# First feed-forward layer of a DiT step: row chunks of the modulation weights on two DMA queues, squares per token, and four weight tiles multiplied part by part

## The chip, the cores and the metric

One core of a Trainium2 chip runs the whole kernel. The metric is the device time of one execution in microseconds (us). The engines named below are TensorE (PE in the views, with PEld for its weight loads), VectorE (DVE), ScalarE (ACT), GpSimd (POOL) and SyncE (SP). SP and ACT also issue DMAs: SP on queue q1, ACT on queue q10. Both queues use the same 16 DMA engines.

## The reference, cut to what matters

One layer is computed for 128 prompt tokens and 512 sample tokens, 640 in all, of width 1024. The change touches only its start: the modulation vectors, the first norm, and the first products of the first feed-forward network. The two groups of tokens have their own conditioning (`c_ctx` and `c`), so every modulation value exists twice.

```python
def adaln(cond, w_ada, b_ada):                     # w_ada: 1024 x 9216, nine vectors of 1024
    m = jax.nn.silu(cond) @ w_ada + b_ada
    return m.reshape(cond.shape[:-1] + (1, N_MOD, D_MODEL))

def modulated_norm(x, gain, shift, scale):
    return rmsnorm(x, gain) * (1 + scale) + shift  # rmsnorm: x * rsqrt(mean(x*x) + EPS) * gain

x = x + 0.5 * mod[..., 2, :] * swiglu(modulated_norm(x, norm_ffn1, mod[..., 0, :], mod[..., 1, :]),
                                      w_ffn1_in, w_ffn1_out)
```

The first norm needs only the modulation vectors 0 and 1 (shift and scale), which are the first 2048 columns of `w_ada`, 8 MB. `swiglu` multiplies the result with `w_ffn1_in` (1024 x 5632: 22 gate and 22 up tiles of 128 columns) and then with `w_ffn1_out`.

## The kernel before, in words

Tokens lie in the free dimension: `x_t` is [128, 8, 640], eight blocks of 128 features (`KD` = 8) by 640 tokens (`T`), and a half is 320 tokens (`HT`). Each fp32 product is made of three matmuls of rounded parts (`w_lo`·`h_hi`, `w_hi`·`h_lo`, `w_hi`·`h_hi`), lines 2234 to 2236, the function `product`. A weight tile [128, 1024] is loaded into `w_raw` (two buffers), ACT rounds it to `w_hi` (`w_high`, line 718) and DVE subtracts to get `w_lo` (`w_low`, line 1330). A part of the norm is one feature block of one half; there are 16. For each part DVE multiplies by the root (`scale_x`, line 1367), ACT applies scale and shift (`modulate`, line 770), and DVE splits the result (`split_h`, lines 1376 and 1377).

The order on each engine is the order in which the code is written, and engines meet only through semaphores. At the start it is this:

- SP issues twelve small loads (lines 509 to 515: identity, biases, conditioning, gains), then `x_tok` (lines 516 and 517), then `w_ada` in column pieces: ten `ada_tiles` of 128 columns and three `ada_wide` of 256 columns, each over all 1024 rows (lines 523 and 525), then the first weight tiles (line 531).
- PE turns the small rows, turns the 40 blocks of `x_tok` into `x_t` (line 2527; ACT copies them out, line 993), multiplies the ten `ada_tiles` with the conditioning (function `ada`, line 2281), sums the squares over features with a matmul by 1/D (`mean`, line 2254), sums the partitions of the three `ada_wide_acc` (`ada_sum`, line 2290), and turns the rows of modulation values into columns (line 2543).
- DVE multiplies the three wide pieces (`ada_setup`, lines 1460 and 1464) and adds up the squares between the first and the second (`add_square`), then makes `w_low` of tiles 0 and 1, `mods` (line 1771) and `scales` (line 1358).
- ACT copies `x_t` out, squares it by feature block (`square_of`, line 725), takes the root (`root`, lines 742 and 744), and makes `w_high` of tiles 0 and 1 and the copies `ada_row` (line 1005).

Then the 16 parts run, and PE multiplies tiles 0 and 1 part by part as they come (`by_parts`). Tiles 2 and 3 get their `w_high` and `w_low` at parts 9 and 15, in slots of their own at the end of the space of `act_lo`. PE multiplies them whole afterwards (`hidden(1, ...)`), and goes on with tiles 4, 5 and so on. Beside it DVE and ACT make the activation of pair `j` (function `hidden` on both), and DVE multiplies two pieces of `w_ada` per pair for the later modulation vectors (`ada_part`, `ada_fold`).

Of the kernel before, what the change touches and what calls it, by code (L numbers as in the profile page):

```python
# [14 lines left out]
P = 128  # L15
# [63 lines left out]
ADA_PE, ADA_DVE = 10, 3  # L79
SQ_BASE, PART_BASE = [0, 8, 12, 16], [None, 0, 4]  # L80
# [185 lines left out]
def hybrid_step(nc, x_prompt, x_sample, cache_diff_k, cache_diff_v, state_delta, c, c_ctx, w_ada, b_ada,  # L266
# [4 lines left out]
    with ctx:  # L271
# [43 lines left out]
        with ExitStack() as s:  # L315
            tb = holder(s)
            x_tok = tb("x_tok", [P, NT, D])

            ada_tiles = [tb(f"ada_tile{i}", [P, D]) for i in range(ADA_PE)]
            ada_row = tb("ada_row", [2, ADA_PE * P])  # L320
            ada_wide = [tb(f"ada_wide{i}", [P, 2 * D]) for i in range(ADA_DVE)]
            rows_a = tb("rows_a", [120, P])
            rows_b = tb("rows_b", [62, P])
        with ExitStack() as s:
            holder(s)("act_space", [P, 2 * NJ * T])
            ada_wide_acc = [holder(s)(f"ada_wide_acc{i}", [P, 2 * PAIR]) for i in range(ADA_DVE)]
        with ExitStack() as s:
# [10 lines left out]
            fold = tb("fold", [P, P])  # L338
            ada_sums = rstd
# [103 lines left out]
        ada_landed = [sem(f"ada_landed{i}") for i in range(ADA_PE)]  # L443
        ada_wide_in = [sem(f"ada_wide_in{i}") for i in range(ADA_DVE)]
        ada_wide_read, ada_rows = sem("ada_wide_read"), sem("ada_rows")
# [55 lines left out]

        @block.sync
        def _(sp):
# [12 lines left out]
            sp.dma_start(x_tok[:, 0, :], x_prompt[0]).then_inc(x_in, 16)  # L516
            sp.dma_start(x_tok[:, 1:NT, :], x_sample[0].rearrange("(t p) d -> p t d", p=P)).then_inc(x_in, 16)
            ada_v = w_ada[0].rearrange("(k p) n -> p k n", p=P)

            for n in range(ADA_PE):  # L520
                if n % 3 == 0 and n // 3 < ADA_DVE:
                    col = ADA_PE * P + n // 3 * PAIR
                    sp.dma_start(ada_wide[n // 3][:].rearrange("p (k n) -> p k n", k=KD),
                                 ada_v[:, :, col:col + PAIR]).then_inc(ada_wide_in[n // 3], 16)
                sp.dma_start(ada_tiles[n][:].rearrange("p (k n) -> p k n", k=KD),  # L525
                             ada_v[:, :, n * P:(n + 1) * P]).then_inc(ada_landed[n], 16)

# [182 lines left out]
        def _(act):  # L710
# [272 lines left out]

            act.wait_ge(cols_turned, 2)
# [4 lines left out]
            nc.scalar.activation(cond[:, :, 0], cols_a[:, 80:88], ACT.Silu).then_inc(cond_ready, 1)  # L989
            for i in range(2 * NT):  # L990
                t, q = i // 2, i % 2
                act.wait_ge(x_turned, i + 1)
                nc.scalar.copy(x_t[:, 4 * q:4 * q + 4, t * P:(t + 1) * P], heads4(ps[:, 2 + i % 4, :], P)).then_inc(x_copied, 1)
            act.wait_ge(x_copied, 2 * NT)
            load_power_table()
            for k in range(KD):
                square_of(k, 0, None)
            root(0, 0)
            root(0, 1)
            w_high(0, 0)  # L1000
            w_high(1, 1)
            act.wait_ge(ada_used, ADA_PE)
            for n in range(0, ADA_PE, 4):
                end = min(n + 4, ADA_PE)
                ins = nc.scalar.copy(ada_row[:, n * P:end * P], ps[0:2, 4 + n // 4, 0:(end - n) * P])
            ins.then_inc(ada_rows, 1)
            for s in range(16):
                modulate(0, s)
                if s in (9, 15):
                    i = 2 if s == 9 else 3  # L1010
                    w_high(i, i % 2, slot=i, done=0)
# [311 lines left out]
        def _(dve):  # L1323
# [63 lines left out]
            def update_half(nth, i, gate, half):  # L1387
# [9 lines left out]
                elif nth == 1 and half == 0:  # L1397
                    dve.wait_ge(half_done[0], i + 1)
                    if i == 0:
                        dve.wait_ge(ada_summed, ADA_DVE + 3)  # L1400
# [97 lines left out]
            def first_ffn():  # L1498

                def hidden(j, par, first=False):  # L1500
# [9 lines left out]
                    if isinstance(j, int) and j == NJ - 1:  # L1510
                        dve.wait_ge(ada_summed, ADA_DVE + 2)
# [245 lines left out]
            def ada_setup(i):  # L1757
                dve.wait_ge(ada_wide_in[i], 16)
                ada_terms(ada_wide_acc[i], ada_wide[i], range(KD), 0, KD - 1).then_inc(ada_wide_read, 1)

            dve.wait_ge(cond_ready, 2)
            ada_setup(0)
# [7 lines left out]
            dve.wait_ge(ada_summed, ADA_DVE + 1)  # L1770
            own.link(nc.vector.tensor_tensor(mods[:, 0:2 * KD, :], ps[:, 7, 0:4 * KD].rearrange("p (m a) -> p m a", a=2),
                                             spread(cols_a[:, 0:2 * KD], 2), ALU.add))
# [3 lines left out]
            for s in range(16):  # L1776
# [3 lines left out]
                if s in (9, 15):  # L1780
                    i = 2 if s == 9 else 3
                    w_low(i, i % 2, slot=i)
# [446 lines left out]
        def _(pe):  # L2229
# [17 lines left out]
            def mean(nth, half):  # L2247

                if nth == 0:
                    pe.wait_ge(sq_added, SQ_BASE[1])  # L2250
                else:
                    pe.wait_ge(added_half[half], PART_BASE[nth] + len(PARTS[nth]))
                bank = half if nth == 0 else 4 + half
                nc.tensor.matmul(ps[:, bank, 0:HT], ones_d[:], half_of(sumsq, half), start=True, stop=True).then_inc(mean_mm, 1)
# [22 lines left out]
            def ada(n):  # L2277

                pe.wait_ge(ada_landed[n], 16)
                for a in range(KD):  # L2280
                    ins = nc.tensor.matmul(ps[0:2, 4 + n // 4, (n % 4) * P:(n % 4 + 1) * P], cond[:, a, :],
                                           ada_tiles[n][:, a * P:(a + 1) * P], start=(a == 0), stop=(a == KD - 1))
                ins.then_inc(ada_used, 1)

            def ada_sum(bank, at, acc):

                for u in range(2):
                    for g in range(2):
                        c = at + 2 * u + g
                        ins = nc.tensor.matmul(ps[:, bank, c:c + 1], acc[:, g * PAIR + u * P:g * PAIR + (u + 1) * P],  # L2290
                                               ones_col[:], start=True, stop=True)
                ins.then_inc(ada_summed, 1)
# [6 lines left out]
            def first_ffn():  # L2299
# [65 lines left out]
                by_parts(0, [0, 1], [0, 1], False)  # L2365
                hidden(1, 1, 2)
# [619 lines left out]
```

## Time and profile before

| | us |
|---|---|
| runs before | 1584.05, 1586.75, 1586.85 |
| median of them | 1586.75 |
| the profiled execution | 1581.51 |
| its span in the trace | 1579.7 |
| PE busy in the span | 1523.3 (96%) |
| DVE, ACT, POOL busy | 1062.2, 591.4, 196.2 |
| moved by DMA | 141.96 MB, of it 118.26 MB on SP's queue |

The profile is of one execution on the chip. Its span is 1.8 us shorter than that execution's time, and that execution is 5.2 us shorter than the median. Times below count from the span's start. PE is busy nearly throughout, so the span is PE's work plus the time in which PE waits. Engines other than PE count where PE waits for them.

### The profile page before, as it was taken

Reading aid. Unit: us, or ns where it says so; the run is one execution under the profiler, and the core shown is the slowest. Engines: PE = TensorE matmul, PEld = TensorE weight load, DVE = VectorE, ACT = ScalarE, POOL = GpSimd, SP = SyncE. Lnnn points to the kernel's source line nnn. Section 1 sums busy time; section 2 is a strip of 40 time slices with the busy share of each in tenths; the row PEclk is TensorE's granted clock in tenths of the full one; section 3 lists DMA queues with packets and bytes.
Section 4 is the critical chain, followed back from the end, with each engine's and each line's share of the span. In section 5 each row is a group of like instructions: output and inputs, shape, how many; then the busy total and the mean of one; then the engine's idle time right before and its main releaser. Section 6 shows DMA issues by size and latency. Waiting matters only on the chain.

```text
span 1579.7 us, 26562 instructions
## 1 busy us (share of the span) xinstructions
PE 1523.3 (96%) x10204; PEld 1435.9 (91%) x10204; DVE 1062.2 (67%) x1908; ACT 591.4 (37%) x1138; POOL 196.2 (12%) x158
## 2 busy tenths in 40 slices
PE   6899999999999999998998999999999999999998
PEld 4899999999999999987887988999999999998886
DVE  5978777787374767554867887678887777763334
ACT  4522222221122533533653214264554444444323
POOL 0000000000000000020006677566000000000000
PEclk9999999999999999999997999999999999999999
DMA  9354454544244312211001101002213322222222
GB/s 303 118 158 142 140 158 148 156 143 157 83 138 147 94 54 67 68 46 49 28 28 34 41 15 28 21 28 83 65 41 94 94 80 80 80 80 67 72 75 94
DMA packets 186937, 141.96 MB, mean 90 GB/s; under 512 B 8544, under 2 KB 169829, under 8 KB 186725
## 3 DMA queue, kind: packets, MB, share of 16 engines
q1 hardware_dynamic: 164149, 118.26, 24.4%
q10 hardware_dynamic: 22704, 22.55, 4.5%
q8 instruction: 57, 0.93, 0.2%
q14 instruction: 27, 0.22, 0.1%
HBM read 137.34 MB, written 3.45 MB: 89 GB/s over the span
## 4 chain that ended last, share of the span: by engine, by line
PE 86%; DVE 7%; SPq 2%; ACT 2%; issue 1%; POOL 1%; DMA 1%; DVEq 0%; ACTq 0%
PE ps L2234 14%; PE ps L2236 14%; PE ps L2235 14%; PE ps L2396 5%; PE ps L2398 5%; PE ps L2397 5%; PE ps L2468 3%; PE ps L2467 3%; PE ps L2466 3%; PE ps L2898 3%; PE ps L2902 3%; SPq L525 2%; PE ps L2669 1%; PE ps L2905 1%; PE ps L2690 1%
## 5 line engine op out<-in xcount | busy, mean ns | idle before, releaser
L2234 PE MATMUL ps<-h_hi,w_lo 128*128 128x320 f32 x1152 | 364.0, 316 | 9.3 <-DVE h_lo L1377 4.0
L2236 PE MATMUL ps<-h_hi,w_hi 128*128 128x320 f32 x1152 | 356.4, 309 | 0.0
L2235 PE MATMUL ps<-h_lo,w_hi 128*128 128x320 f32 x1152 | 356.4, 309 | 0.0
L1330 DVE TENSOR_TENSOR w_lo<-w_raw,w_hi 128x1024 fp32r<-128x1024 f32 x120 | 147.6, 1233 | 232.0 <-ACT w_hi L718 231.7
L2234 PEld LDWEIGHTS ps<-h_hi,w_lo 128*128 128x128 f32 x1152 | 216.9, 188 | 15.9 <-DVE h_lo L1377 6.9
L2235 PEld LDWEIGHTS ps<-h_lo,w_hi 128*128 128x128 f32 x1152 | 217.1, 188 | 0.8 <-issue 0.2
L2236 PEld LDWEIGHTS ps<-h_hi,w_hi 128*128 128x128 f32 x1152 | 216.7, 188 | 0.0
L718 ACT CAST w_hi<-w_raw 128x1024 fp32r<-128x1024 f32 x120 | 125.6, 1048 | 207.1 <-PE ps L2236 109.5
L1464 DVE SCALAR_TENSOR_TENSOR ada_acc<-ada_ffn,cond,ada_acc 128x256 f32<-128x256 f32 x392 | 161.8, 478 | 1.2
L2234 PE MATMUL ps<-act_hi,w_lo 128*128 128x320 f32 (+1 forms) x352 | 108.9, 309 | 2.1 <-DVE mods L1493 2.1
L2236 PE MATMUL ps<-act_hi,w_hi 128*128 128x320 f32 (+1 forms) x352 | 108.5, 308 | 0.0
L2235 PE MATMUL ps<-act_lo,w_hi 128*128 128x320 f32 (+1 forms) x352 | 108.5, 308 | 0.0
L2396 PE MATMUL ps<-h_hi,w_lo 128*128 128x320 f32 x304 | 94.0, 309 | 0.6 <-ACT sumsq L882 0.6
L2398 PE MATMUL ps<-h_hi,w_hi 128*128 128x320 f32 x304 | 93.9, 309 | 0.0
L2397 PE MATMUL ps<-h_lo,w_hi 128*128 128x320 f32 x304 | 93.7, 308 | 0.0
L2466 PE MATMUL ps<-w_hi,act_hi 128*128 128x512 f32 x220 | 87.4, 397 | 0.0
L2468 PE MATMUL ps<-w_hi,act_lo 128*128 128x512 f32 x220 | 86.8, 395 | 0.0
L2467 PE MATMUL ps<-w_lo,act_lo 128*128 128x512 f32 x220 | 86.8, 394 | 0.0
L812 ACT CAST act_hi<-scratch 128x640 f32 (+1 forms) x22 | 16.0, 728 | 148.2 <-DVE scratch L1519 148.2
L2234 PEld LDWEIGHTS ps<-act_hi,w_lo 128*128 128x128 f32 x352 | 66.1, 188 | 2.4 <-issue 2.3
L2235 PEld LDWEIGHTS ps<-act_lo,w_hi 128*128 128x128 f32 x352 | 66.1, 188 | 0.1
L2236 PEld LDWEIGHTS ps<-act_hi,w_hi 128*128 128x128 f32 x352 | 66.1, 188 | 0.0
(384 smaller groups left out, 3200.4 us busy)
## 6 DMA issues: line engine op xcount, KB each, us to landing
w_raw<-in_w_ffn_in SPq DMA_DIRECT2D x64, 512.0 KB, 3.8
w_raw<-in_w_ffn_out SPq DMA_DIRECT2D x44, 512.0 KB, 3.7
ada_ffn<-in_w_ada ACTq DMA_DIRECT2D x43, 512.0 KB, 3.5
w_raw<-in_w_in SPq DMA_DIRECT2D x28, 512.0 KB, 3.7
ada_ffn<-in_w_ffn_in SPq DMA_DIRECT2D x20, 512.0 KB, 3.7
ada_ffn<-in_w_ada SPq DMA_DIRECT2D x13, 512.0 KB, 4.5
ada_tile<-in_w_ada SPq DMA_DIRECT2D x10, 512.0 KB, 7.8
w_raw<-in_w_out SPq DMA_DIRECT2D x8, 512.0 KB, 3.4
```

The costliest lines, as they stand in the source:

```text
L718: nc.scalar.copy(w_hi[s if slot is None else slot], w_raw[s][:]).then_inc(w_hi_ready, 1)
L1330: nc.vector.tensor_tensor(w_lo[at], w_raw[s][:], w_hi[at].bitcast(F32), ALU.subtract)\
L1464: ins = nc.vector.scalar_tensor_tensor(a, w, col, a, op0=ALU.mult, op1=ALU.add)
L2234: nc.tensor.matmul(out, lo, xh, start=start, stop=False)
L2235: nc.tensor.matmul(out, hi, xl, start=False, stop=False)
L2236: return nc.tensor.matmul(out, hi, xh, start=False, stop=stop)
L2396: nc.tensor.matmul(out, lo, xh, start=start and k == 0, stop=False, skip_group_check=not start)
L2397: nc.tensor.matmul(out, hi, xl, start=False, stop=False, skip_group_check=not start)
L2398: ins = nc.tensor.matmul(out, hi, xh, start=False, stop=k == 3, skip_group_check=not start)
L2466: nc.tensor.matmul(out, lo, wh, start=first, stop=False)
L2467: nc.tensor.matmul(out, hi, wl, start=False, stop=False)
L2468: ins = nc.tensor.matmul(out, hi, wh, start=False, stop=last)
```

## The change

The loads. `w_ada` is now read in eight chunks of 128 rows by 2048 columns (`ada_k`, `head_load`), 1 MB each, so that one row of a chunk is 8 KB in one piece. ACT issues chunks 0, 1 and 2, then `x_tok`, then chunk 3, ahead of all its other work. SP issues the twelve small loads as before, then chunk 4, `fold`, weight tile 0, chunk 5, weight tile 1, chunks 6 and 7.

The modulation values. Of every chunk PE multiplies the first 1152 columns (`ada`, three matmuls per chunk, summed in PSUM over the chunks), and DVE the other 896 (`ada_chunk`, two instructions per chunk). One transposing reduction on DVE and one matmul by `fold` take the place of the 12 matmuls by `ones_col`.

The norm. The squares are taken per token from `x_tok` with a sum along the row (five instructions), the root is five columns, and six matmuls of a broadcast column with the identity (`HEAD_SPREAD`) spread it over the partitions; ACT copies it to `rstd`.

The products. `first_parts(4)` multiplies four weight tiles: at step `s` tiles 0 and 1 with part `s`, tiles 2 and 3 with part `s - 4`. `hidden(1, ...)` is gone. `w_high` and `w_low` of tiles 2 and 3 stand at parts 1 and 2 of ACT, 2 and 3 of DVE, where they stood at 9 and 15.

```diff
@@ sync: before                                    @@ after
-            sp.dma_start(x_tok[:, 0, :], x_prompt[0]).then_inc(x_in, 16)
-            sp.dma_start(x_tok[:, 1:NT, :], x_sample[0].rearrange("(t p) d -> p t d", p=P)).then_inc(x_in, 16)
...
+            for k in range(4, KD):
+                head_load(sp, k)
+                if k == 4:
+                    sp.dma_start(fold[:], consts[:, N_SMALL:N_SMALL + P]).then_inc(fold_in, 16)
+                if k in (4, 5):
+                    ffn_load(k - 4)
+            for i in range(2, 4):
+                ffn_load(i)
@@ scalar
+            for k in range(3):
+                head_load(act, k)
+            act.dma_start(x_tok[:, 0, :], x_prompt[0]).then_inc(x_in, 16)
+            act.dma_start(x_tok[:, 1:NT, :], x_sample[0].rearrange("(t p) d -> p t d", p=P)).then_inc(x_in, 16)
+            head_load(act, 3)
...
+            for t in range(NT):
+                ins = nc.scalar.activation(x_tok[:, t, :], x_tok[:, t, :], ACT.Square, accum_out=tok_rs[:, t:t + 1])
...
             w_high(0, 0)
+            for half in range(2):
+                act.wait_ge(mean_mm, half + 1)
+                nc.scalar.copy(half_of(rstd, half), ps[:, half, 0:HT]).then_inc(rstd_ready, 1)
             w_high(1, 1)
@@ vector
             for k in range(KD):
-                add_square(k, 0)
-            ada_setup(1)
-            ada_setup(2)
-            w_low(0, 0)
-            w_low(1, 1)
+                ada_chunk(k)
+                if k in (4, 5):
+                    w_low(k - 4, k - 4)
+            own.wait_back(0)
+            nc.vector.tensor_reduce(head_sums[:], ada_wide_acc[:].rearrange("p (n r) -> p n r", r=32), AX.X, ALU.add,
+                                    apply_transpose=True).then_inc(ada_wide_read, 1)
@@ tensor
+            def first_parts(lag):
+                for s in range(2 * KD + lag):
+                    for m in range(4):
+                        p = s if m < 2 else s - lag
+                        if not 0 <= p < 2 * KD:
+                            continue
+                        half, k = divmod(p, KD)
+                        if m == 0:
+                            pe.wait_ge(h_ready, p + 1)
+                        if p == 0:
+                            pe.wait_ge(w_lo_ready, m + 1)
...
-                by_parts(0, [0, 1], [0, 1], False)
-                hidden(1, 1, 2)
+                first_parts(4)
...
+            pe.wait_ge(cond_ready, 2)
+            for a in range(3):
+                ada(a)
             pe.wait_ge(x_in, 32)
             for i in range(2 * NT):
                 t, q = i // 2, i % 2
-                if i >= 4:
-                    pe.wait_ge(x_copied, i - 3)
+                if i in (7, 9):
+                    ada(3 if i == 7 else 4)
+                if i >= len(HEAD_BANKS):
+                    pe.wait_ge(x_copied, i - len(HEAD_BANKS) + 1)
```

Where instructions stand. On DVE at the start, of the kernel before: the wide pieces, the sums of squares between them, and both `w_lo` after them, ahead of `mods`.

```order
L1460 TENSOR_SCALAR ada_wide_acc<-ada_wide,cond 128x256 x2
L1464 SCALAR_TENSOR_TENSOR ada_wide_acc<-ada_wide,cond,ada_wide_acc 128x256 x14
L1339 COPY sumsq<-square 128x640
L1342 TENSOR_TENSOR sumsq<-sumsq,square 128x640 x7
...
L1330 TENSOR_TENSOR w_lo<-w_raw,w_hi 128x1024 x2
L1771 TENSOR_TENSOR mods<-ps,cols_a 128x32
```

On DVE at the start, of the changed kernel, from the first chunk to the first `scratch` of the norm:

```order
L1779 TENSOR_SCALAR ada_wide_acc<-ada_k,cond 128x896 x2
L1782 SCALAR_TENSOR_TENSOR ada_wide_acc<-ada_k,cond,ada_wide_acc 128x896 x8
L1345 TENSOR_TENSOR w_lo<-w_raw,w_hi 128x1024
L1782 SCALAR_TENSOR_TENSOR ada_wide_acc<-ada_k,cond,ada_wide_acc 128x896 x2
L1345 TENSOR_TENSOR w_lo<-w_raw,w_hi 128x1024
L1782 SCALAR_TENSOR_TENSOR ada_wide_acc<-ada_k,cond,ada_wide_acc 128x896 x4
L1791 TENSOR_REDUCE head_sums<-ada_wide_acc 128x56
L1795 TENSOR_TENSOR mods<-ps,cols_a 128x18
L1801 TENSOR_TENSOR mods<-ps,cols_a 32x14 x4
L1373 SCALAR_TENSOR_TENSOR scales<-mods,cols_a 128x16
```

The two `w_lo` have moved from behind the last wide piece to between chunks 4 and 5 and between chunks 5 and 6, so three chunks and the reduction now stand behind the first of them. The sums of squares are gone from DVE.

On ACT at the start, of the changed kernel, from the issue of its six loads to the copies `ada_row`; each wait is in brackets. Before, its first row was the copy `cols_a`, and the squares stood behind ten copies of `x_t` as here.

```order
L506 DMA ada_k<-in_w_ada 128x2048 x3
L989 DMA x_tok<-in_x_prompt 128x1024
L990 DMA x_tok<-in_x_sample 128x4x1024
L506 DMA ada_k<-in_w_ada 128x2048
...
L1002 COPY x_t<-ps 128x4x128 [waits x_turned] x10
L1005 ACTIVATE x_tok,tok_rs<-x_tok 128x1024 [waits x_turned]
L1005 ACTIVATE x_tok,tok_rs<-x_tok 128x1024 x4
L1010 ACTIVATE tok_rs<-tok_rs,eps_col 128x5 [waits ones_set,sq_tok]
L1012 ACTIVATE tok_rs<-tok_rs 128x5 [waits log_ready]
L722 CAST w_hi<-w_raw 128x1024 [waits w_landed0]
L1016 COPY rstd<-ps 128x320 [waits mean_mm] x2
L722 CAST w_hi<-w_raw 128x1024 [waits w_landed1]
```

The load of `x_tok` has moved from SP to ACT and stands behind three chunks of 1 MB. The first `w_hi`, for which the first `w_lo` on DVE waits, stands behind the squares and the root, as it did before.

## Rows read from the trace of the kernel before

**Rows 1.** Windows, three stretches: start:end, length, busy (instructions), PEclk, DMA share, GB/s.

```profile
0.00:48.14 48.14, 30.00 (x241) 24.10 (x241) 29.13 (x68) 22.48 (x38) 0.21 (x4) 0.96 0.86 275
48.14:67.46 19.32, 17.94 (x97) 15.42 (x98) 18.72 (x46) 13.66 (x23) 0.00 (x0) 0.93 0.28 90
67.46:1579.70 1512.24, 1475.35 (x9870) 1396.39 (x9868) 1014.32 (x1796) 555.23 (x1078) 195.98 (x154) 0.99 0.27 84
```

**Rows 2.** Chain of waits of the start: start, length, what.

```profile
35.23 6.50 DMA w_raw<-in_w_ffn_in
```

**Rows 3.** Timeline, SP: start, length, issue.

```profile
0.75 0.38 SPq L509 DMA_DIRECT2D ident<-in_consts  x1
...
4.63 0.25 SPq L515 DMA_DIRECT2D rows_b<-in_diff_norm  x1
4.93 0.36 SPq L516 DMA_DIRECT2D x_tok<-in_x_prompt  x1
```

**Rows 4.** Timeline, PE: start, length, instruction, [idle before it, released by].

```profile
5.89 0.46 PE L2519 MATMUL ps<-ident,rows_a 120*128 120x120 f32 x1 [5.89 <-DMA rows_b<-in_diff_norm]
...
13.77 6.06 PE L2527 MATMUL ps<-ident,x_tok 128*128 128x128 f32 x40 [7.13 <-DMA x_tok<-in_x_sample]
21.03 8.89 PE L2281 MATMUL ps<-ada_tile,cond 128*2 128x128 f32 x80 [1.20 <-ACT x_t L993]
```

**Rows 5.** Windows, DMA rate of two stretches: `x_tok`, then column pieces of `w_ada`.

```profile
8.00:14.00 6.00, 0.23 (x1) 0.23 (x2) 0.00 (x0) 0.66 (x3) 0.00 (x0) 1.00 1.02 401
17.00:29.00 12.00, 10.80 (x100) 8.82 (x98) 11.20 (x22) 10.74 (x17) 0.00 (x0) 1.00 1.13 359
```

**Rows 6.** Timeline, ACT at the start.

```profile
8.48 0.19 ACT L989 ACTIVATE cond<-cols_a 128x8 f32<-128x8 f32 x1
...
16.63 4.14 ACT L993 COPY x_t<-ps 128x512 f32<-128x512 f32 x8 [0.27 <-PE ps L2527]
...
41.75 1.04 ACT L718 CAST w_hi<-w_raw 128x1024 fp32r<-128x1024 f32 x1 [0.43 <-DMA w_raw<-in_w_ffn_in]
```

**Rows 7.** Groups by form, ACT, whole run: busy us, mean ns | idle before.

```profile
L754 ACT ACTIVATE square<-x_fin 128x512 f32<-128x512 f32 x10 | 6.3, 629 | 4.9 <-DVE x_fin L1445 4.6
...
L754 ACT ACTIVATION_READ_ACCUMULATOR square<-x_fin 128x1 f32 x10 | 1.9, 186 | 0.0
...
L1315 ACT ACTIVATE sums_fin<-sums_fin 128x1 f32<-128x1 f32 x5 | 1.5, 295 | 0.5
```

**Rows 8.** Timeline, DVE at the start.

```profile
17.13 5.63 DVE L1464 SCALAR_TENSOR_TENSOR ada_wide_acc<-ada_wide,cond,ada_wide_acc 128x256 f32<-128x256 f32 x14
...
41.94 2.35 DVE L1330 TENSOR_TENSOR w_lo<-w_raw,w_hi 128x1024 fp32r<-128x1024 f32 x2
45.37 0.19 DVE L1771 TENSOR_TENSOR mods<-ps,cols_a 128x32 f32<-128x32 f32 x1 [1.08 <-PE ps L2543]
```

**Rows 9.** Groups by form, DVE, whole run.

```profile
L1798 DVE SCALAR_TENSOR_TENSOR conv_acc<-pre,cols_b,conv_acc 128x642 f32<-128x642 f32 x48 | 42.6, 888 | 5.2 <-DVE conv_acc L1798 3.3 <-DVE conv_acc L1796 1.1
...
L1464 DVE SCALAR_TENSOR_TENSOR ada_wide_acc<-ada_wide,cond,ada_wide_acc 128x256 f32<-128x256 f32 x42 | 16.9, 480 | 0.0
...
L1484 DVE TRANSPOSE_TENSOR_REDUCE rstd<-ada_acc 128x16 f32<-128x512 f32 x12 | 8.5, 712 | 0.4
```

**Rows 10.** Timeline, PE: first products, and tile 2 at its start and eight products later.

```profile
48.14 0.64 PE L2234 MATMUL ps<-h_hi,w_lo 128*128 128x320 f32 x1 [2.88 <-DVE h_lo L1377]
...
50.97 0.31 PE L2235 MATMUL ps<-h_lo,w_hi 128*128 128x320 f32 x1
...
67.46 0.31 PE L2234 MATMUL ps<-h_hi,act_lo 128*128 128x320 f32 x1
...
70.97 0.31 PE L2234 MATMUL ps<-h_hi,act_lo 128*128 128x320 f32 x1
```

**Rows 11.** Timeline, DVE after the norm: activation of pair 0.

```profile
72.26 0.81 DVE L1519 TENSOR_TENSOR scratch<-square,ps 128x640 f32<-128x640 f32 x1
...
76.03 2.35 DVE L1330 TENSOR_TENSOR w_lo<-w_raw,w_hi 128x1024 fp32r<-128x1024 f32 x2
```

More of the change, by code:

```diff
@@ L325, in hybrid_step @@
             holder(s)("act_space", [P, 2 * NJ * T])
-            ada_wide_acc = [holder(s)(f"ada_wide_acc{i}", [P, 2 * PAIR]) for i in range(ADA_DVE)]
+            ada_wide_acc = holder(s)("ada_wide_acc", [P, 2 * ADA_WIDE * P])
         with ExitStack() as s:
@@ L992, in _ @@
                 act.wait_ge(x_turned, i + 1)
[L993 to L999, printed above, removed]
+                nc.scalar.copy(x_t[:, 4 * q:4 * q + 4, t * P:(t + 1) * P], heads4(ps[:, HEAD_BANKS[i % len(HEAD_BANKS)], :], P)).then_inc(x_copied, 1)
+            act.wait_ge(x_turned, 2 * NT)
+            for t in range(NT):
+                ins = nc.scalar.activation(x_tok[:, t, :], x_tok[:, t, :], ACT.Square, accum_out=tok_rs[:, t:t + 1])
+            ins.then_inc(sq_tok, 1)
+            act.wait_ge(sq_tok, 1)
+            act.wait_ge(ones_set, 1)
+            rs = tok_rs[:, 0:NT]
+            nc.scalar.activation(rs, rs, ACT.Ln, bias=eps_col[:], scale=1.0 / D).then_inc(log_ready, 1)
+            act.wait_ge(log_ready, 1)
+            nc.scalar.activation(rs, rs, ACT.Exp, scale=-0.5).then_inc(log_ready, 1)
             w_high(0, 0)
+            for half in range(2):
+                act.wait_ge(mean_mm, half + 1)
+                nc.scalar.copy(half_of(rstd, half), ps[:, half, 0:HT]).then_inc(rstd_ready, 1)
             w_high(1, 1)
-            act.wait_ge(ada_used, ADA_PE)
             for n in range(0, ADA_PE, 4):
                 end = min(n + 4, ADA_PE)
+                act.wait_ge(ada_used, n // 4 + 1)
                 ins = nc.scalar.copy(ada_row[:, n * P:end * P], ps[0:2, 4 + n // 4, 0:(end - n) * P])
@@ L1008, in _ @@
                 modulate(0, s)
-                if s in (9, 15):
-                    i = 2 if s == 9 else 3
-                    w_high(i, i % 2, slot=i, done=0)
+                if s in (1, 2):
+                    w_high(s + 1, (s + 1) % 2, slot=s + 1, done=0)
             first_ffn()
@@ L1773, in _ @@
+            dve.wait_ge(ada_summed, HEAD_SUMS)
+            for q in range(4):
+                rows = slice(32 * q, 32 * q + 32)
+                sums = ps[rows, 3, 0:8 * ADA_WIDE].rearrange("p (g u q) -> p u g q", g=2, q=4)[:, :, :, q]
+                own.mark(nc.vector.tensor_tensor(mods[rows, ADA_PE:2 * KD, :], sums, spread(cols_a[rows, ADA_PE:2 * KD], 2), ALU.add))
+            own.wait_back(0)
             make_scales(0)
@@ L2275, in by_parts, with ada @@
                             mean(nth, 1)
[L2277 to L2292, printed above, removed]
+            def first_parts(lag):
[9 more added lines that the diff above has]
+                            pe.wait_ge(w_lo_ready, m + 1)
+                        w = (w_hi[m][:, k * P:(k + 1) * P], w_lo[m][:, k * P:(k + 1) * P])
+                        x = [half_of(h[k // 4][:, k % 4, :], half) for h in (h_hi, h_lo)]
+                        ins = product(ps[:, 2 * m + half, 0:HT], k, w, x, k == 0, k == KD - 1)
+                        if p == 2 * KD - 1:
+                            ins.then_inc(tile_done, 1)
+            def ada(a):
+                pe.wait_ge(ada_landed[a], 16)
+                for i, n in enumerate((512, 512, ADA_PE * P - 1024)):
+                    ins = nc.tensor.matmul(ps[0:2, 4 + i, 0:n], cond[:, a, :], ada_k[a][:, i * 512:i * 512 + n],
+                                           start=(a == 0), stop=(a == KD - 1))
+                    if a == KD - 1:
+                        ins.then_inc(ada_used, 1)
             def ada_fold(col, i0, i1):
@@ L2544, in _ @@
             ins.then_inc(ada_summed, 1)
+            pe.wait_ge(fold_in, 16)
+            pe.wait_ge(ada_wide_read, 1)
+            nc.tensor.matmul(ps[:, 3, 0:8 * ADA_WIDE], fold[:], head_sums[:], start=True, stop=True).then_inc(ada_summed, 1)
             first_ffn()
```

95 lines of the change are left out of this document (46 added, 49 removed).

## The prediction

> **What bounds the kernel now.** I cut the span into stretches first. From 67.46 on PE is busy 1475 of 1512 us [rows 1], and the change leaves that stretch's work alone except for the first pairs. Before 48.14 PE is busy 30 us, but none of it is a product; from 48.14 to 67.46 it multiplies tiles 0 and 1. So the question is by how much the first product at 48.14, and then the start of tile 4, come earlier or later. I call the first product's time F.
>
> The chain of waits says what sets F today: SP's queue. It ends on the landing of weight tile 1, which `w_hi` waits for until 41.75 [rows 2, 6]. From 8 to 14 us the queue delivers 401 GB/s with the DMA engines full (share 1.02), and from 17 to 29, in pieces of 512 B and 1 KB, 359 GB/s with a share of 1.13 [rows 5]. Before the first product 12.1 MB must land: 8.39 of `w_ada`, 2.62 of `x_tok`, 1.05 of two weight tiles. `x_tok` stands in front and has landed at 13.77 [rows 4]. Not far behind the queue is DVE, which works without a gap from 17.1 to 44.3 [rows 8].
>
> **What the change gives in bytes.** 8 KB rows are nearest to the 4 KB rows of `x_tok`, so I take 401 GB/s for everything. 12.1 MB is then 30.2 us. A load's lead (issue, first byte, last receipt) is what `x_tok` shows: issued at 4.93, landed at 13.77, 8.84 us for 6.54 us of bytes, so 2.3 us [rows 3, 4]. ACT's first issue can stand at 0.75, like SP's today. All would have landed at about 33.5 instead of 41.7. The Trainium skill ("DMA: Bandwidth & Descriptors", section "Issuing engines are not separate DMA queues") says that DMAs of two engines interleave on the same 16 DMA engines and that a second issuer saves only issue time. The share of 1.02 on one queue [rows 5] agrees, and the 33.5 already counts one bandwidth for both queues.
>
> **What it costs in order.** If only bytes counted, F would come from the last chunk: two DVE instructions, the reduction, the fold, `mods` and the first part, near 41. But `x_tok` no longer stands in front. I call its landing X and follow what hangs on it.
>
> 1. *Copies.* From X to the last copy of `x_t` takes 7.0 us today (13.77 to 20.77, [rows 4, 6]). PE now also multiplies chunks 3 and 4 between the blocks: 40 products of 128 columns take 8.89 us, 0.222 each, so 9 x 0.222 = 2.0 us a chunk [rows 4]; ACT's backlog hides some 0.5 of the 4.0. X + 10.5.
> 2. *Squares.* Five of 1024 columns. One of 512 takes 0.63, and reading its sum 0.19 [rows 7]; a cast of 1024 takes 1.04 [rows 6], twice the 512 would be 1.26. I take 1.05 + 0.19 less 0.1 of overlap, 1.14 each, 5.7 in all (5.2 to 7.2). X + 16.2.
> 3. *Root.* Two instructions on five columns, 0.30 and below [rows 7], with hand-overs 0.65. X + 16.85.
> 4. *`w_high(0)`*: 1.04 [rows 6]. X + 17.9. It was hidden behind loads before.
>
> On DVE the wait that matters is new: `w_low(0)` waits for this `w_high(0)`, and behind it on DVE stand chunks 5, 6 and 7, `w_low(1)`, the reduction, `mods` and the norm. PE waits for the norm. Their prices:
>
> 5. Two `w_low`, 2.35 [rows 8].
> 6. Three chunks, six instructions of 896 columns. 256 columns take 0.480, 642 take 0.888 [rows 9], so 1.06 ns a column and 1.16 for 896; back to back 14 of 256 take 5.63, 0.40 each [rows 8, 9], 0.08 less than alone. 6 x 1.08 = 6.5.
> 7. The reduction: 0.71 for 512 columns [rows 9]; with the same slope 2.1 for 1792 (1.9 to 2.5).
> 8. The fold matmul with hand-overs, 0.4, an estimate: 56 columns are under the 0.22 of 128 [rows 4].
> 9. From `mods` at 45.37 to the first product at 48.14 it takes 2.77 today [rows 8, 10]; four more small additions cost 0.4 (one takes 0.19 alone). 3.2.
> 10. Hand-overs on DVE, 0.3.
>
> Together 14.85, so **F = X + 32.7**. `w_high(1)`, the `rstd` copies and `ada_row` lie beside steps 5 and 6. `w_low(1)` needs `w_high(1)` about 2.2 after `w_high(0)`, and DVE comes to it 3.4 after. Chunk 0 to 4's work on DVE lies in front of the wait and costs nothing, nor do the additions of squares that went.
>
> **X.** Ahead of it and in it on ACT's queue are 3.15 + 2.62 = 5.77 MB. No stretch of this trace has two full queues, so I bound it. If ACT's queue is served alone: 0.75 + 2.3 + 14.4 = 17.4. If both queues get the same bytes from 7.2 on, when chunk 4 (issued in `x_tok`'s old place at 4.93) flows, 1.67 MB have gone and 4.1 MB take 20.5 us: 27.7. Between: both queues take turns row by row. Chunk rows are 8 KB, rows of `x_tok` 4 KB, rows of a weight tile 512 B. ACT's 1.5 MB of chunks then goes beside chunk 4's 1.05 MB; after it SP's small rows take little, about 0.35 MB of `fold` and tile 0. X = 17.4 + 1.4/0.401 = 20.9. I take 20.9: it needs no rank among the queues and lies between the bounds, nearer to the one with ACT's head start. F = 53.6, 5.5 later than 48.14.
>
> **Four tiles.** Today tiles 0 and 1 end at 67.46, and a product takes 0.439 (eight from 67.46 to 70.97), so tiles 2 and 3 end at 81.5, F + 33.4 [rows 10]. A part comes every 1.2 us (16 in 19.3, [rows 1]) and PE, with two products of 0.88 each, waits for it. After: parts 2 and 3 carry both `w_low` (2.35) and ACT's two `w_high`, so part 4 comes at about F + 7.3, with eight products done; its waits hide the slow start, in which today ten matmuls take 2.83 instead of 1.47 [rows 10]. From there four products a step, 1.76, outlast the norm's 1.2, and the other 56 products take 24.6: F + 31.9. Then tile 4. Its `w_low` stands on DVE behind the activation of pair 0, and from there to its end took 72.26 to 77.2, 4.95 us [rows 11]. Today a whole pair of tiles (14 us) covers it. Now tiles 0 and 1 end only at about F + 27.6; with 0.4 until DVE can start, `w_lo` is there at F + 33.0, and PE waits 1.1. Net 0.4 gained, nought to 2 in the range.
>
> **Sum.** 5.5 - 0.4 = 5.1 later. The profiled execution would take 1581.5 + 5.1 = 1586.6. The median stands 5.2 above it, and I carry that over: 1586.75 + 5.1 = 1591.9, so 1592.
>
> **Rivals.**
> - *ACT's queue goes first* (no change). Place: the 16 DMA engines between 7 and 21 us. If chunk 4 and tile 0 don't hold `x_tok` up, X = 17.4 and F = 50.1; 2.0 - 0.4 = 1.6 later, 1588.4. It decides below X = 18.9, where the loss is 3.2. For it: ACT's loads are all issued by 3.5, before SP's big ones. Against it: nothing in the trace gives one queue a rank.
> - *Equal bytes.* X = 27.7, and chunk 3, which PE wants at X + 4, lands with the last of SP's at 33 and costs 1.3 more. F = 61.7: 13 later, 1600.
> - *The small loads come late.* SP's twelve small loads, landed at 5.89 today [rows 4], now meet a full ACT queue. If each of them waits behind a chunk, they land with ACT's 6.8 MB, near 20; `cond` is ready 2.8 after them (8.67, [rows 4, 6]), PE multiplies chunks 0 to 2 for 6 us ahead of the blocks, and X counts as 28: F = 60.7, 12 later, 1599. The Trainium skill ("DMA: Bandwidth & Descriptors", section "Queues, rings and completion order") says that each DMA engine goes round the queues packet by packet, a packet being some 9 to 17 descriptors; a chunk has 8 rows per DMA engine, so by that rule this rival holds. No run here shows it, and the sum above does without it.
> - *Faster.* X = 17.4, the short squares (0.5), the short reduction (0.2) and 2 us from four tiles together: F = 49.4, and 0.7 us gained, 1586. More than that needs a price that I have wrong: the wait of `w_low(0)` gone, which would leave the bytes as the bound, F near 41 and 1579.
>
> **How the numbers follow.** A measurement of this kernel tells 0.2%, 3.2 us, from no change. Row by row 0.44 (1592), ACT first 0.20 (1588.4, no change), small loads late 0.13 (1599), equal bytes 0.13 (1600), faster cases 0.10, of which 0.02 lie within 3.2. That gives slower 0.70, same 0.22, faster 0.08. The range runs from 1585 to 1601: it leaves out most of the faster cases and the upper end of equal bytes.
>
> **What would show it.** In the changed profile: `x_tok` lands between 17 and 28, and PE's idle time before its blocks names it. DVE idles before the first `w_lo`, released by ACT's `w_hi`, though chunk 5 has landed. The first product comes near X + 33. There is a short PE gap before tile 4, released by DVE's `w_lo`. I am wrong if DVE goes through `w_lo` without idling, if `x_tok` lands before 16, or if F is below 48.

## The result, and the profile after

The changed kernel takes 1588.27 us (median of 12 runs, 1586.33 to 1592.33), the kernel before 1586.13 (12 runs, 1582.52 to 1588.37). The ratio of the runs is 1.0025, 95% interval 1.0015 to 1.0035: 4.0 us slower, 2.4 to 5.6; the two medians by themselves lie 2.1 apart. That lies in the forecast range and on the forecast side. The profiled execution took 1586.57 with a span of 1584.8, 5.1 us more than before. The sum had said 5.1.

TensorE's own row first, the timeline of PE after (start, length, instruction, idle before it and who ended it). It answers [rows 4, 10]: the small rows turned, the chunks multiplied, the blocks of `x_tok`, the fold, the first product, part 4 and tile 4.

```profile
11.67 0.46 PE L2553 MATMUL ps<-ident,rows_a 120*128 120x120 f32 x1 [11.67 <-DMA rows_b<-in_diff_norm]
...
14.51 7.69 PE L2324 MATMUL ps<-ada_k,cond 128*2 128x512 f32 x18 [2.08 <-ACT cond L997]
22.13 3.27 PE L2566 MATMUL ps<-ident,x_tok 128*128 128x128 f32 x28
...
49.39 0.65 PE L2585 MATMUL ps<-head_sums,fold 128*128 128x56 f32 x2 [5.29 <-DVE head_sums L1791]
53.41 0.63 PE L2263 MATMUL ps<-h_hi,w_lo 128*128 128x320 f32 x1 [3.38 <-DVE h_lo L1392]
60.61 0.41 PE L2263 MATMUL ps<-h_hi,w_lo 128*128 128x320 f32 x1 [0.86 <-DVE h_lo L1392]
86.65 0.41 PE L2263 MATMUL ps<-h_hi,w_lo 128*128 128x320 f32 x1 [1.14 <-DVE w_lo L1345]
```

F is 53.41 (forecast 53.6), part 4 stands at F + 7.2 (7.3), tile 4 at F + 33.2 (33.0) behind a gap of 1.14 (1.1). Before, tile 4 started at 81.54, so the start costs 5.1 us. The span is 5.1 longer: nothing behind tile 4 adds to it or gives it back.

The loads, as the groups of DMA issues after (KB each, us from issue to landing). ACT issued the prompt at 2.17 and the sample at 2.90:

```profile
x_tok<-in_x_sample ACTq DMA_DIRECT2D x1, 2048.0 KB, 17.6
...
x_tok<-in_x_prompt ACTq DMA_DIRECT2D x1, 512.0 KB, 12.5
```

X, the landing of `x_tok`, is 20.5 (forecast 20.9; before 13.77). The bytes go as fast as hoped, by the windows after (start:end, length, busy of PE, PEld, DVE, ACT, POOL, then PEclk, DMA share, GB/s), which answer [rows 5]:

```profile
8.00:12.00 4.00, 0.33 (x1) 0.18 (x1) 0.00 (x0) 0.00 (x0) 0.00 (x0) 1.00 1.02 426
20.00:24.00 4.00, 4.00 (x26) 2.38 (x24) 0.72 (x2) 1.18 (x3) 0.00 (x0) 1.00 1.04 402
...
28.00:32.00 4.00, 3.32 (x16) 1.15 (x14) 0.00 (x0) 1.97 (x4) 0.00 (x0) 1.00 1.01 428
32.00:36.00 4.00, 3.78 (x12) 0.85 (x10) 0.00 (x0) 4.00 (x9) 0.00 (x0) 1.00 0.07 31
```

From 32 on the queues are nearly empty: the last load, chunk 7, landed at 33.2, where before the last one landed at 41.7. DVE could have gone on. Its timeline after shows why it didn't, and answers [rows 8]:

```profile
38.42 1.23 DVE L1345 TENSOR_TENSOR w_lo<-w_raw,w_hi 128x1024 fp32r<-128x1024 f32 x1 [10.78 <-ACT w_hi L722]
39.57 2.21 DVE L1782 SCALAR_TENSOR_TENSOR ada_wide_acc<-ada_k,cond,ada_wide_acc 128x896 f32<-128x896 f32 x2
41.69 1.22 DVE L1345 TENSOR_TENSOR w_lo<-w_raw,w_hi 128x1024 fp32r<-128x1024 f32 x1
42.83 4.33 DVE L1782 SCALAR_TENSOR_TENSOR ada_wide_acc<-ada_k,cond,ada_wide_acc 128x896 f32<-128x896 f32 x4
47.20 2.04 DVE L1791 TRANSPOSE_TENSOR_REDUCE head_sums<-ada_wide_acc 128x56 f32<-128x1792 f32 x1
```

It stood 10.78 us before the first `w_lo`, released by ACT's `w_hi`, and only then took chunks 5 to 7, which had landed at 26.6, 30.7 and 33.2. The chain of waits after (start, length, what) tells where `w_hi` was held, and here is the surprise:

```profile
5.14 6.49 DMA rows_b<-in_diff_norm
14.51 7.69 PE ps L2324 x18
22.20 3.21 PE ps L2566 x28
...
31.59 5.31 ACT x_tok L1005 x10
```

The chain runs back through the squares and the blocks, as forecast, but not to `x_tok`. It runs to the 18 products of chunks 0 to 2, which PE does ahead of the blocks, and from there to the twelve small loads. PE began the blocks at 22.13, 1.6 us after `x_tok` had landed, without a wait for it. The idle time of PE that the prediction named as a sign of `x_tok`'s landing isn't there.

### The profile page after: what moved, and what is told of

Same layout as the page of the kernel before. It is cut to its first block, busy times and chain, and to the rows that moved or that the text cites. A ratio compares the mean times of both kernels' runs of the same rounds, so it can differ in the third digit from the quotient of the medians.

```text
span 1584.8 us, 26270 instructions
## 1 busy us (share of the span) xinstructions
PE 1522.2 (96%) x10077; PEld 1425.8 (90%) x10077; DVE 1057.0 (67%) x1873; ACT 589.9 (37%) x1140; POOL 196.2 (12%) x158
## 4 chain that ended last, share of the span: by engine, by line
PE 87%; DVE 7%; ACT 2%; issue 2%; POOL 1%; DMA 1%; SPq 0%; DVEq 0%; ACTq 0%
PE ps L2263 14%; PE ps L2265 14%; PE ps L2264 14%; PE ps L2430 5%; PE ps L2432 5%; PE ps L2431 5%; PE ps L2500 3%; PE ps L2501 3%; PE ps L2502 3%; PE ps L2939 3%; PE ps L2943 3%; PE ps L2710 1%; PE ps L2946 1%; PE ps L2731 1%; PE ps L2855 1%
```

## The experiments

Theory: the wait of `w_lo` for `w_hi`, put ahead of three chunks on DVE, turns ACT's late chain into time, and the late chain begins at X. Rivals: the bytes set F; or PE's own order does, whatever X is. Where a ratio is given, the kernel ran 11 or 12 times; the others ran once, and for those the moments in the profile count and not the total. F of one program in two profiles differed by 0.74 in one case and 0.25 in another.

**Both `w_lo` behind the reduction.**

```
                 ada_chunk(k)
-                if k in (4, 5):
-                    w_low(k - 4, k - 4)
             ...tensor_reduce(head_sums...)
+            w_low(0, 0)
+            w_low(1, 1)
```

> One edit to the changed kernel: on VectorE both w_low (tiles 0 and 1) move from between chunks 4, 5 and 6 to behind the transposing reduction. Nothing else. Order theory (chunks 5 to 7 stand in the queue behind a w_low that waits for ScalarE's w_high at 38.4): VectorE works through chunk 7 as it lands (about 32) and has reduced by 37.4; w_low 0 ends at 39.6, w_low 1 at 42.2; mods then waits for the turned ada_row at 44.1; first product at 48.0, 5.4 earlier than the 53.41 of the changed kernel, and as early as before (48.14). Span 1579.4, ratio to before 0.9985 to 1.000. Bytes theory (the first product hangs on the landing of the chunks and on what follows the last one): first product within 1 us of 53.4, span 1584 to 1585.

The reduction on DVE in this kernel, then its first product on PE:

```profile
35.53 2.05 DVE L1789 TRANSPOSE_TENSOR_REDUCE head_sums<-ada_wide_acc 128x56 f32<-128x1792 f32 x1
```

```profile
47.19 0.64 PE L2263 MATMUL ps<-h_hi,w_lo 128*128 128x320 f32 x1 [3.38 <-DVE h_lo L1392]
```

F came to 47.19, 6.2 us earlier, and tile 4 to 80.41 (F + 33.2). DVE reached the reduction at 35.53 instead of 47.20. The blocks began at 23.11 here, 1.0 later than in the changed kernel, so the order of `w_lo` on DVE cost more than those 6.2 us: from the start of the blocks to F takes 24.08 here and 31.28 there, 7.2 less. The whole run shows less: 1584.66 us, ratio 1.0001 (0.9987 to 1.0014), span 1582.8, only 2.0 under the changed kernel's. The windows of this kernel show where the profiled execution lost the rest:

```profile
719.00:723.00 4.00, 2.04 (x15) 1.62 (x13) 0.92 (x5) 3.73 (x9) 0.00 (x0) 1.00 0.02 4
723.00:727.00 4.00, 3.90 (x15) 3.68 (x15) 2.59 (x9) 0.39 (x3) 0.00 (x0) 0.50 0.44 127
727.00:731.00 4.00, 3.48 (x13) 3.08 (x13) 0.00 (x0) 1.13 (x5) 0.00 (x0) 0.50 0.01 4
731.00:735.00 4.00, 3.96 (x21) 3.12 (x19) 1.66 (x8) 0.12 (x1) 0.00 (x0) 0.72 0.00 0
```

PE was idle for half of 719 to 723, and then ran until 733 at a granted clock of 0.50, the lower level. In the changed kernel the same place has the same idle time and the full clock behind it:

```profile
725.00:729.00 4.00, 2.28 (x17) 1.85 (x15) 0.69 (x4) 3.66 (x7) 0.00 (x0) 1.00 0.02 4
729.00:733.00 4.00, 3.15 (x18) 2.71 (x19) 2.82 (x10) 1.48 (x8) 0.00 (x0) 1.00 0.40 113
```

By the copies `v_b` (719.32 here, 725.55 there) this kernel was 6.2 us ahead, by the next group (741.87 and 744.05) only 2.2. The clock took 4.0 us, far behind the edit. Whether the edit has a part in that, three later kernels ask (below).

**`x_tok` first on ACT's queue, and its blocks first on PE.**

```
-            for k in range(3):
-                head_load(act, k)
             act.dma_start(x_tok[:, 0, :], x_prompt[0]).then_inc(x_in, 16)
...
-            head_load(act, 3)
+            for k in range(4):
+                head_load(act, k)
...
-            pe.wait_ge(cond_ready, 2)
-            for a in range(3):
-                ada(a)
             pe.wait_ge(x_in, 32)
...
-                if i in (7, 9):
-                    ada(3 if i == 7 else 4)
+                if i == 3:
+                    pe.wait_ge(cols_ready, 2)
...
             pe.wait_ge(x_copied, 2 * NT)
-            ada(5)
-            ada(6)
+            pe.wait_ge(cond_ready, 2)
+            for a in range(3):
+                ada(a)
             pe.wait_ge(log_ready, 2)
...
-            ada(7)
+            for a in range(3, KD):
+                ada(a)
```

> The changed kernel with ScalarE issuing x_tok ahead of chunks 0 to 3, and TensorE turning the 40 blocks ahead of chunks 0 to 2, the spread of the root behind chunk 2. VectorE's order, with both w_low between the chunks, is kept. Order theory: x_tok lands at about 10 to 12, squares end near 24, the first w_low is ready when VectorE reaches it near 29, so VectorE doesn't idle before it; what is left is the landing of chunk 7 (32 to 33.5) and VectorE's own work: first product at 42 to 44.5, span 1574 to 1576, ratio to before 0.994 to 0.998. Rival (the row chunks and the token-wise norm are the loss, wherever x_tok stands): first product 50 or later, ratio above 1.

```profile
11.35 7.14 PE L2562 MATMUL ps<-ident,x_tok 128*128 128x128 f32 x40
...
43.16 0.63 PE L2262 MATMUL ps<-h_hi,w_lo 128*128 128x320 f32 x1 [3.38 <-DVE h_lo L1391]
```

F was 43.16, tile 4 at 76.40, 1577.77 us, ratio 0.9961 (0.9948 to 0.9974): faster than both kernels. The span is 1576.2, 8.6 us under the changed kernel's, though tile 4 came 10.2 earlier: from 361 to 365 the granted clock was 0.57 here, behind two us of idle PE, where the changed kernel has the same idle time and 1.00. `w_lo` stands where the changed kernel has it, and DVE did not idle before it. What it waited for now is the bytes:

```profile
27.53 1.22 DVE L1344 TENSOR_TENSOR w_lo<-w_raw,w_hi 128x1024 fp32r<-128x1024 f32 x1
...
30.79 1.22 DVE L1344 TENSOR_TENSOR w_lo<-w_raw,w_hi 128x1024 fp32r<-128x1024 f32 x1
...
34.95 2.21 DVE L1781 SCALAR_TENSOR_TENSOR ada_wide_acc<-ada_k,cond,ada_wide_acc 128x896 f32<-128x896 f32 x2 [0.82 <-DMA ada_k<-in_w_ada]
```

So the theory of the wait holds. This kernel has two edits, though; the next three take them apart.

**ACT's queue alone until `x_tok` is in.**

```
+            sp.wait_ge(x_in, 32)
             for k in range(4, KD):
                 head_load(sp, k)
```

> The changed kernel with SyncE waiting for x_tok before it issues chunk 4 and all that follows, so that ScalarE's queue has the DMA engines to itself after the twelve small loads. Row-by-row theory (SyncE's large loads take their turns and hold x_tok up): x_tok's second load lands at 17.4 to 18 instead of 20.5, the blocks start at 19 to 20 instead of 22.1, the first product comes 2 to 3 us earlier than 53.4, since chunk 7 (33 to 34) is not what VectorE waits for. Rival (ScalarE's queue is served first anyway, and something else makes 20.5): x_tok lands at 20 or later. If the small loads are late because of ScalarE's chunks alone, they still land at 11 to 12 here; if SyncE's own large loads delay them, earlier.

`x_tok` landed at 17.2 (issued at 2.9, 14.3 us), where the rival "ACT's queue goes first" had put it. F did not follow: 54.20, span 1585.7, 1587.53 us. PE after that edit:

```profile
11.76 0.46 PE L2554 MATMUL ps<-ident,rows_a 120*128 120x120 f32 x1 [11.76 <-DMA rows_b<-in_diff_norm]
...
14.60 8.38 PE L2325 MATMUL ps<-ada_k,cond 128*2 128x512 f32 x18 [2.08 <-ACT cond L998]
22.91 3.28 PE L2567 MATMUL ps<-ident,x_tok 128*128 128x128 f32 x28
```

The blocks waited 5.7 us beside landed data, for PE's 18 products ahead of them. My expectation, that F would come earlier, failed, and with it X as the one origin of F. The small loads were as late as before though SP's big loads were gone: it is ACT's loads that hold them up.

**The order of the loads alone** (`x_tok` first, PE as in the changed kernel).

> The changed kernel with one edit: ACT issues x_tok ahead of chunks 0 to 3; PE's order as in the changed kernel. Theory (PE's own order sets F: the 18 products of chunks 0 to 2 stand ahead of the blocks, and they wait for the small loads, the conditioning and now for chunk 2 near 20.5): the blocks start at 22 to 23 though x_tok has landed before 12, F 53 to 54, span 1584 to 1586. Rival (F is the landing of x_tok plus 32.7, as in the sum of the prediction): F 43 to 45.

`x_tok` landed at 10.7, ten us earlier than in the changed kernel, and F was 54.84, as late as in the changed kernel or later, as the theory had it (span 1586.5, 1588.27 us): chunk 0 now holds PE until 15.20, and the 18 products take 8.44.

```profile
15.20 8.44 PE L2323 MATMUL ps<-ada_k,cond 128*2 128x512 f32 x18 [3.25 <-DMA ada_k<-in_w_ada]
23.56 3.28 PE L2565 MATMUL ps<-ident,x_tok 128*128 128x128 f32 x28
```

**The order on PE alone** (blocks first, loads as in the changed kernel).

> The changed kernel with the other edit alone: PE turns the blocks of x_tok ahead of all products of chunks; the order of the loads as in the changed kernel. Theory: the blocks start with the landing of x_tok, 20.5, and without two chunks between them take 7.2 to the last copy: w_hi ends near 34.8 instead of 38.4, F 49.5 to 50, span 1581. Rival (the landing of x_tok alone sets it, the order on PE costs nothing): F 53.4. With both edits together F was 43.2, so each alone should give less than half of the 10.2 us.

```profile
20.60 6.93 PE L2563 MATMUL ps<-ident,x_tok 128*128 128x128 f32 x40 [7.93 <-DMA x_tok<-in_x_sample]
```

Now the blocks do wait for `x_tok`, until 20.60, and F was 50.74, 2.7 us earlier (span 1582.1, 1583.85 us). It is 0.7 later than expected: DVE's `mods` now waited 1.22 for the rows that PE turned at 46.29, behind five chunks' products. One edit alone gives 2.7 us, the other loses 1.4, both together give 10.2: the load's place pays only once PE takes the blocks first.

**Both, and both `w_lo` behind the reduction.**

> The version with x_tok ahead of the chunks and the blocks first on PE, and in addition both w_lo on DVE behind the transposing reduction. Theory (in this order the landing of chunk 7 near 35 sets F, and w_lo has become cover that costs nothing ahead of it): the two w_lo, 2.4 us, move behind the landing, of which about 0.5 hides in the wait for the fold matmul: F 45.0 against 43.2, a span near 1578. Rival (the wait of w_lo for w_hi is the cost in every order): F no later than 43.2, span 1576 or less.

F was 44.83 against 43.16, 1.7 us worse; 1582.68 us, span 1580.9, with a granted clock of 0.50 from 723 to 731 too. DVE after that edit:

```profile
34.95 2.21 DVE L1781 SCALAR_TENSOR_TENSOR ada_wide_acc<-ada_k,cond,ada_wide_acc 128x896 f32<-128x896 f32 x2 [1.72 <-DMA ada_k<-in_w_ada]
37.20 2.04 DVE L1788 TRANSPOSE_TENSOR_REDUCE head_sums<-ada_wide_acc 128x56 f32<-128x1792 f32 x1
39.17 2.32 DVE L1344 TENSOR_TENSOR w_lo<-w_raw,w_hi 128x1024 fp32r<-128x1024 f32 x2
```

The same move that gave 6.2 us of F costs 1.7 here, since the landing of chunk 7 comes last and the two `w_lo` had filled time in which DVE waited.

**Products of a constant ahead of the chunks**, to keep PE busy: 20 ahead of the wait for the small loads, 8 behind the rows.

```
+            pe.wait_ge(ones_set, 1)
+            for n in range(20):
+                nc.tensor.matmul(ps[:, 2, 0:P], ones_d[:], ones_d[:], start=True, stop=True)
             pe.wait_ge(small_in, 16 * 12)
...
+            for n in range(8):
+                nc.tensor.matmul(ps[:, 2, 0:P], ones_d[:], ones_d[:], start=True, stop=True)
```

> The changed kernel with 28 products of a constant tile on PE, whose results nobody reads: 20 ahead of the wait for the small loads, 8 behind the two rows that are turned, where PE stood idle. Theory (the 18 products of chunks 0 to 2 are slow because PE was idle before them, and they, not the landing of x_tok, start the blocks): they take 6.0 us instead of 7.7, the blocks start at 20.5 to 20.7, now with the landing of x_tok, F 51.8 to 52.0, span 1583. Rival (what slows them is something else, such as the reads beside the DMAs that write the chunks): 7.7 to 8.6 us again, blocks at 22.1 or later, F 53.4 or later.

```profile
12.40 3.19 PE L2559 MATMUL ps<-ones_d 128*128 128x128 f32 x16
15.52 6.43 PE L2324 MATMUL ps<-ada_k,cond 128*2 128x512 f32 x18
21.89 3.28 PE L2571 MATMUL ps<-ident,x_tok 128*128 128x128 f32 x28
```

The 18 products took 6.43 instead of 7.69, so idle time ahead of them is most of what slowed them; the last section shows by which way. My 8 extra products, behind 3.66 us of idle PE, ran at a granted clock of 0.64 (12 to 16), ended 1.0 late and ate the gain: blocks at 21.89, F 53.17, 0.24 us earlier. The total says nothing on it (span 1586.2, 1588.01 us): from 371 to 375 the granted clock was 0.57 here and 1.00 in the changed kernel. A step of 0.24 is less than two profiles of one program can differ. What tells more is the distance from the start of the blocks to F, 31.28 here, and 31.28 or 31.29 in every kernel that keeps PE's order and the place of both `w_lo` in the start: the changed one, the two with `x_tok` landed at 17.2 and 10.7, and the one below with four tiles undone. So it was PE's coming to the blocks, not `x_tok`, that came last. The 51.8 was not reached and stays an estimate.

**Four tiles undone** (tiles 0 and 1 by parts, then 2 and 3 whole; their `w_high` and `w_low` back at parts 9 and 15).

> The changed kernel with the part on four weight tiles undone: tiles 0 and 1 part by part, tiles 2 and 3 whole afterwards, their w_high and w_low at parts 9 and 15 as before. Theory of the prediction: the four tiles are worth about 0.4, since the norm is held up by both w_low early and tile 4 waits for its w_low: first product 53.4, tile 4 starts 33.4 after it (86.8 against 86.65), span 1584.5 to 1585.5. Rival (the four tiles save the waits between parts, 3 us or more, and hide that much of the loss): tile 4 starts 36 us or more after the first product of the changed kernel, span 1588 or more.

F was 53.67, span 1585.0, 1586.77 us. The gap before tile 4 is gone, and nothing is won: from F to the pieces of `ada_part` that start at 365.27 it takes 311.60 us, in the changed kernel (364.93) 311.52. Four tiles by parts gain 0.1 us.

**`w_lo` of tile 4 ahead of the last pieces of `ada_part` of pair 0**, on top of the version with both orders.

```
+                    if first and j == 0:
+                        w_low(4, 0)
                     ada_part(j, 1, ada_acc, range(6, 8))
...
-                        w_low(4, 0)
                         w_low(5, 1)
```

> x_tok first on the queue and the blocks first on PE, and in addition w_lo of tile 4 on DVE moved from behind the pieces of ada_part of pair 0 to just behind the product that ends the activation of pair 0. Theory: the wait of PE ahead of tile 4 (1.14 us, released by DVE's w_lo) goes, nothing else moves: tile 4 starts at F + 32.1, span 1575, ratio to the kernel before 0.9955. Rival (the pieces of ada_part that are now late hold up a later wait): the 1.1 us comes back at a wait within the next pairs, span 1576.

```profile
97.53 0.41 PE L2263 MATMUL ps<-h_hi,w_lo 128*128 128x320 f32 x1 [1.17 <-DVE w_lo L1344]
```

The rival was right: the gap left tile 4 and came back as 1.17 us one pair later. At the pieces of `ada_part` near 354 the two versions stand level (354.71 and 354.69). DVE is behind by that much, wherever the wait falls. The kernel took 1578.05 us, ratio 0.9972 (0.9962 to 0.9982), which can't be told from 0.9961.

**The stretch at half clock: the same two kernels again, and a third with `w_lo` in that place.**

> The kernel with both w_lo behind the reduction, once more. The open question is its stretch at a granted clock of 0.50 near 723, which took 4.0 us. If chance decides it, the stretch is missing or elsewhere this time (18.5 us from the copies v_b to the next group of products, a span near 1578.8); if the moment at which PE pauses decides it, v_b starts within 0.5 us of 719.3 again and the stretch is there again (22.5 us).

> x_tok first, blocks first and both w_lo behind the reduction, once more: the other kernel whose profile had the stretch at 0.50. Chance: missing this time, a span near 1577; the moment or the edit: 22.5 us again and a span near 1581. F 44.8 in either case.

> The changed kernel with the blocks first on PE and both w_lo behind the reduction; the order of the loads as in the changed kernel. F between 47 and 50, since PE still has chunks to multiply before it can turn the modulation rows. If the place of w_lo as such brings the stretch at 0.50, it is here too, 22.5 us from v_b to the next group; if the moment or chance does, most likely not, 18.5 us.

From `v_b` to the next group of products the first kernel, the same program as in the first experiment, now took 18.50 us (718.63 to 737.13) instead of 22.55. Its windows:

```profile
719.00:723.00 4.00, 1.94 (x14) 1.46 (x13) 1.60 (x5) 3.43 (x9) 0.00 (x0) 1.00 0.02 4
723.00:727.00 4.00, 3.48 (x23) 3.10 (x23) 1.90 (x9) 1.14 (x5) 0.00 (x0) 1.00 0.46 131
```

F 46.45, tile 4 at 79.69, span 1577.8, 1579.57 us: without the stretch the 7.0 us gained at tile 4 reach the end of the span whole. The second took 22.59 (718.37 to 740.96), with F 44.58, span 1582.0, 1583.75 us. The third took 18.50 (722.98 to 741.48), span 1582.1, 1583.93 us; its F of 50.85 is above the 47 to 50 expected and no better than the 50.74 with `w_lo` in the changed place, since PE turns `ada_row` only at 46.39, behind the chunks it still had to multiply, and `w_lo` is off the path. The times of the twelve runs of the first experiment go with their mean granted clock: five with a mean granted clock of 0.986 took 1586.96 to 1587.67 us, five at 0.989 1582.61 to 1584.71, and two at 0.990 1579.02 and 1579.56. So one program runs with and without the stretch, and `w_lo` behind the reduction does not bring it each time. `v_b` at 718.63 without it stands between 718.37 and 719.32 with it, so that moment alone does not decide either. What does is open.

## Why the prediction was right, and where it was not

The sign, the size and the seat were right: 5.1 in the profiled span, from DVE's wait for `w_hi` at the start. The steps one by one:

- *Bytes.* 401 GB/s assumed, 371 to 428 in windows of 4 us from 4 to 32; all landed at 33.2, forecast 33.5. No bound.
- *X.* 20.9 forecast, 20.5 measured, so the two queues shared about as row by row would have it. The DMA view after says the same of the rule: from 12 to 16 ACT's queue moved 276 packets and SP's 268, from 16 to 20 365 and 364, and nearly every packet in that view is one row. But X did not act: the step "F = X + 32.7" is the one that failed. With X at 17.2 F was 54.20, with X at 10.7 it was 54.84. What held in its place, with the orders of the changed kernel, is F = start of the blocks + 31.28, and that start hung on the small loads and on PE's own order. The rival "ACT's queue goes first" was priced at 50.1, and it would have given nothing.
- *The small loads.* I made them a rival at 0.13 and put them near 20; they came at 11.67, 5.8 us later than before [rows 4]. That, `cond` 2.8 behind it and 7.69 of products ended at 22.13, later than X. The products were put at 6 in that rival; the 1.7 above it are the lower clock of the last section. So this rival's mechanism was at work, with less delay than its price, and I had written its chain down without asking what it gives at 11 instead of 20.
- *Step 1* then ran from 22.13 to 31.69 in 9.6 instead of 10.5. The 1.2 us by which the blocks began later than my X and these 0.9 cancelled. The forecast of `w_hi`'s end, 38.8, met 38.4 by that luck.
- *Steps 2 to 4.* Squares 5.3 (5.7), then the root, `w_hi` 1.03 (1.04).
- *Steps 5 to 10.* From the first `w_lo` to the reduction 8.78 (8.85 without hand-overs), the reduction 2.04 (2.1), from its end to F 4.2 (3.9).
- *Four tiles.* 0.4 gained, in a range from nought to 2; the runs say 0.1.
- *The median.* I carried over the 5.2 us by which the median shown stood above the profiled run. After, that distance was 1.7, and over 12 runs of before the median was 1586.13. This and not the sum is why 1592 is 3.7 above the measured median. The spread between runs of one kernel is of this size; the runs of one program with and without half clock near 723 show one source of it, 4.0 us.

The Trainium skill ("DMA: Bandwidth & Descriptors", section "Queues, rings and completion order") says that an engine drains a whole packet of one queue's ring before it turns to the next queue. The small loads' 11.67 agrees with it in kind: they landed behind ACT's second chunk (8.5), ahead of its third (12.2) and ahead of `x_tok`. The equal numbers of rows agree with turns as well; how many rows make a turn, these windows don't tell. One chunk's wait for each of the twelve, as I had read it, does not hold. With `x_tok`'s 4 KB rows ahead of them instead of 8 KB rows they landed at 10.55 to 11.19 (five kernels), against 11.67 to 12.07 (eight).

## What to carry to other kernels

A wait put between steps of an in-order engine costs what its releaser is late, less what the engine would have waited for anyway: the same two `w_lo` cost 7.2 us in one order of loads and blocks and hid 1.7 in the other, so ask first which of the two comes last. When a load moves, follow what the consuming engine does ahead of it as well: here the load's place was worth nothing until PE took the blocks first, then 10.2 us with it.

## What the runs showed of the hardware

Eighteen products that took 5.97 us behind the blocks took 7.53 to 8.57 behind an idle PE; with products of a constant ahead of them it was 6.43. Those of the changed kernel, from 14.6 to 17.8 and from 18.3 to 19.8 (shortest, median and longest in ns):

```profile
L2324 PE MATMUL ps<-ada_k,cond x4: 1015/1061/1061, 14.5 to 17.0; 128*2 128x512 f32 x4
L2324 PE MATMUL ps<-ada_k,cond x5: 273/592/592, 18.1 to 19.4; 128*2 128x512 f32 x4, 128*2 128x128 f32 x1
```

The first matmuls of 512 columns start 0.85 us apart, the later ones 0.43: half the pace until 18.0, the lower of the clock's two levels, and the full pace behind it. In the kernel with products of a constant the trace's record of the clock reaches further back, and there a matmul of 512 columns under 0.50 (at 15.52) took 1011 ns too. The column of the granted clock reads 1.00 in both stretches, but the record of the clock has its first entry at 18.0 here, so ahead of that the column is no reading. In six profiles the 18 products took 5.97 plus half the time from their start to that first entry, within 0.04 us. The Trainium skill ("TensorE: Matmul & The Clock Gate", section "Part 1: The HAM clock gate") says that the throttled clock is the default and activity lifts it. The durations agree with that.

The same two us of idle PE near 720 were followed by some ten us at 0.50 in three of the profiles (F 47.19, 44.83 and 44.58) and by none in the others, one of them of the same program (F 46.45). Such a stretch takes 4.0 us, as much as the whole difference that was to be measured.

Chunks with 8 KB rows moved 426 GB/s beside a second queue (8 to 12) and 428 on SP's queue alone (28 to 32, when ACT's last load had landed at 23.3), where one queue with 4 KB rows had moved 401 and with pieces of 512 B and 1 KB 359 [rows 5]. These windows show no gain in rate from a second queue.
